# Rotary low pass of the attention scores on half the array's rows, two key chunks at a time

## The chip, the cores and the metric

One core of a Trainium2 chip runs the whole program. The metric is the device time of one execution in microseconds (us). TensorE (PE, with its weight loads PEld listed apart), VectorE (DVE), ScalarE (ACT), GpSimd (POOL) and SyncE (SP) each run their own instruction stream in order and wait for one another by semaphores.

## What is computed

The reference is a two-layer backbone over 2048 latent tokens with a prefix of 256 context tokens. Layer 0 is multi-head latent attention with 8 heads, layer 1 a Conformer convolution module. Only the scores of layer 0 matter here:

```python
NOPE_DIM, ROPE_DIM = 128, 64
q = jnp.concatenate([q_nope, q_rope], axis=-1)      # 128 + 64
k = jnp.concatenate([k_nope, k_rope], axis=-1)      # k_rope: one for all heads
s = jnp.einsum('bhqd,bhkd->bhqk', qi, k).astype(jnp.float32) * scale
p = jax.nn.softmax(s, axis=-1)
o = jnp.einsum('bhqk,bhkd->bhqd', p, v)
```

There are 2304 keys (2048 latent and 256 context) and 2048 queries for each head.

## The kernel before

The kernel works in fp32r, a reduced fp32 form, and splits each operand into a high part and a low part (what the high part leaves over); a product is then high by high, high by low and low by high. `attention` runs over 8 heads h, for each over 4 blocks j of 512 queries, and in each block over 4 query tiles i of 128. I call one (h, j) a phase. The 2304 keys are 5 chunks c: four of 512 and a last one of 256; each has its own PSUM bank `S[:, c]`.

`scores` (L831 to L848) fills one bank with five passes: three for the 128 plain dimensions (L843 to L845), and two for the rotary 64. For the latter `qr` holds the high part of the rotary query on partitions 0 to 63 and its low part on 64 to 127, and `krhi` and `krlo` hold the rotary key twice, once on each half. The pass L847, `qr` by `krhi`, thus gives high by high and low by high at once, and L848, `qr` by `krlo`, gives high by low and low by low. L848 increments `s_qk`, which says that the chunk is complete.

Phase (h, j) on TensorE makes the scores of the next phase's tile i while it transposes and multiplies the probabilities of its own. The list `slots` holds 18 key tiles and one entry `den` (the softmax denominators), and `cuts` gives 5, 5, 4 and 5 of them to the four tiles. `step` is one such entry: four transposes into one of two banks `T` (L874) and the three passes of the value product into `O` for the entry two before (L95 to L97, in the helper `split3`; the first phase's last and `den` have none). After the scores of chunk 0, 1 and 2 (only 0 and 1 in tile 2) comes one step each, and after chunk 4 two more. In tile 0 the value product of entry 0 follows chunk 3. In tile 1 a one-column product (L904) stands ahead of chunk 4.

The waits around it: `scores` of chunk c waits for `s_exp`, that is until ScalarE has taken the exponential of the previous tile's chunk c out of the same bank. `transposes` waits for `s_lo` of the entry two before, since VectorE has to have read that `T` bank.

VectorE (`phase` in its own stream) takes per tile, in this order: the maximum of chunk 0 (L1091, waits for `s_qk`), `low` of the step behind it (L1125, the low part of the transposed probabilities), the maximum of chunk 1, `low`, then the denominator of the tile before (L1110, L1112, L1117; in tile 0 the output L1134 ahead of it), the maximum of chunk 2, `low`, the maxima of chunks 3 and 4, the maximum of the five (L1098) and its negated, scaled form `nmax` (L1102); in tile 1 `q_low` follows, and then the two `low` of the tile's last two steps. ScalarE makes the high parts (`high`, L1004), waits for `nmax`, and takes the five exponentials (L988) with two `high` among them. `q_high` (L975, L976) splits the queries two phases ahead, in tile 1, and increments `s_qhi` twice.

Of the kernel before, what the change touches and what calls it, by code (L numbers as in the profile page):

```python
# [26 lines left out]
F32 = mybir.dt.float32  # L27
F32R = mybir.dt.float32r
ALU = mybir.AluOpType
ACT = mybir.ActivationFunctionType  # L30
AXX = mybir.AxisListType.X

P = 128
# [4 lines left out]
BLK = 512  # L38
NBLK = SEQ // BLK
HEADS, NOPE, ROPE, VDIM = 8, 128, 64, 128  # L40
# [11 lines left out]
NCHUNK = 5  # L52
# [6 lines left out]
def chunk(c):  # L59
    return slice(c * BLK, min((c + 1) * BLK, TOK))  # L60
# [628 lines left out]
def attention(nc, net):  # L689
# [12 lines left out]
    with nc.cleanup_on_exit(), ExitStack() as st:  # L702
        sb = lambda n, s, d=F32: st.enter_context(nc.sbuf_tensor("at_" + n, s, d))
# [5 lines left out]
        krhi, krlo = sb("krhi", [P, TOK], F32R), sb("krlo", [P, TOK], F32R)  # L709
        qst, qrst = sb("qst", [P, 2, BLK]), sb("qrst", [P, 2, BLK])  # L710
        qhi, qlo = sb("qhi", [P, 2, BLK], F32R), sb("qlo", [P, 2, BLK], F32R)
        qr = sb("qr", [P, 2, BLK], F32R)
        pthi, ptlo = sb("pthi", [P, 3, BLK], F32R), sb("ptlo", [P, 3, BLK], F32R)
        mx = sb("mx", [P, 2, 8])
        nmax = sb("nmax", [P, 2])
# [10 lines left out]
        S = st.enter_context(nc.psum_tensor("at_S", [P, NCHUNK, BLK], F32))  # L726
# [21 lines left out]
        def index(h, j):  # L748
            return h * NBH + j
# [80 lines left out]
        def _(pe):  # L830
            def scores(h, j, i, c):  # L831

                b = index(h, j)
                t = b * QT + i
                if i == 0 and c == 0:
                    pe.wait_ge(s_qlo, b + 1)
                if j == 0 and i == 0:
                    pe.wait_ge(s_klo, h * NCHUNK + (c + 1))
                if not (isinstance(t, int) and t == 0):
                    pe.wait_ge(s_exp, (t - 1) * NCHUNK + (c + 1))  # L840
                r, q, k = j % 2, slice(i * P, (i + 1) * P), chunk(c)
                out = S[:, c, 0:k.stop - k.start]
                nc.tensor.matmul(out, qhi[:, r, q], khi[:, k], start=True, stop=False)  # L843
                nc.tensor.matmul(out, qhi[:, r, q], klo[:, k], start=False, stop=False)  # L844
                nc.tensor.matmul(out, qlo[:, r, q], khi[:, k], start=False, stop=False)  # L845

                nc.tensor.matmul(out, qr[:, r, q], krhi[:, k], start=False, stop=False)  # L847
                nc.tensor.matmul(out, qr[:, r, q], krlo[:, k], start=False, stop=True).then_inc(s_qk, 1)  # L848

            def transposes(h, j, n):  # L850

# [55 lines left out]
            def phase(h, j, with_scores=True):  # L907

                nh, nj = (h, j + 1) if j + 1 < NBH else (h + 1, 0)
                for i in range(QT):  # L910
                    ns = list(range(cuts[i], cuts[i + 1]))
                    for c in range(NCHUNK):
                        if i == 1 and c == NCHUNK - 1:
                            modulation_tile(h, j)
                        if with_scores:
                            scores(nh, nj, i, c)
                        if c < len(ns) - TAIL:
                            step(h, j, ns[c])
                        if i == 0 and c == TAIL + 1:
                            values(h, j, 0)  # L920
                    for n in ns[-TAIL:]:
                        step(h, j, n)
# [13 lines left out]
            for i in range(QT):  # L936
                for c in range(NCHUNK):
                    scores(0, 0, i, c)
# [13 lines left out]
        def _(act):  # L952
# [15 lines left out]
            def q_high(h, j):  # L968
                h, j = h + j // NBH, j % NBH
                b, r = index(h, j), j % 2  # L970

                act.wait_ge(s_q[r], h * (48 * NBH // 2) + 48 * (j // 2 + 1))
                if not (isinstance(b, int) and b < 2):
                    act.wait_ge(s_qk, (b - 1) * (QT * NCHUNK))
                nc.scalar.activation(qhi[:, r], qst[:, r], ACT.Copy).then_inc(s_qhi, 1)  # L975
                nc.scalar.activation(qr[:, r], qrst[:, r], ACT.Copy).then_inc(s_qhi, 1)  # L976

            def exponential(h, j, i, c):
                b = index(h, j)
# [31 lines left out]
            def phase(h, j, last=False):  # L1011
# [3 lines left out]
                for i in range(QT):  # L1015
                    ns = list(range(cuts[i], cuts[i + 1]))
                    for c, n in enumerate(ns[:-TAIL]):
                        high(h, j, n)
                        if head_ends and i == QT - 1:
                            k_high(h + 1, c)  # L1020
                        if c == 0:
                            if j == NBH - 1 and not last and i >= 2:
                                v_high(h + 1, i - 2)
                            if j == 0 and i == 1:
                                v_high(h, VC - 1)
                    if i == 1 and (not last or j + 2 < NBH):
                        q_high(h, j + 2)
                    if i == 1 and not (isinstance(h, int) and h == 0 and j == 0):
                        store_output(*((h, j - 1) if j else (h - 1, NBH - 1)))
                    if with_scores:  # L1030
                        exponential(nh, nj, i, 0)
                    high(h, j, ns[-2])
                    if with_scores:
                        exponential(nh, nj, i, 1)
                        exponential(nh, nj, i, 2)
                    high(h, j, ns[-1])
                    if head_ends and i == QT - 1:
                        for c in range(len(ns) - TAIL, NCHUNK):
                            k_high(h + 1, c)
                    if with_scores:  # L1040
                        exponential(nh, nj, i, 3)
                        exponential(nh, nj, i, 4)

            act.wait_ge(s_krin, 16)
            nc.scalar.activation(krhi[:], prob[:, 1, 0], ACT.Copy).then_inc(s_krhi, 1)
            q_high(0, 0)
            for c in range(NCHUNK):
                k_high(0, c)
            for i in range(QT):
                for c in range(NCHUNK):  # L1050
                    exponential(0, 0, i, c)
                if i == 1:
                    q_high(0, 1)
# [14 lines left out]
        def _(dve):  # L1068
# [10 lines left out]
            def q_low(h, j):  # L1079
                h, j = h + j // NBH, j % NBH  # L1080
                b, r = index(h, j), j % 2
                dve.wait_ge(s_qhi, b * 2 + 2)
                nc.vector.tensor_tensor(qlo[:, r], qst[:, r], qhi[:, r].bitcast(F32), ALU.subtract)
                nc.vector.tensor_tensor(qr[ROPE:P, r], qrst[ROPE:P, r], qr[ROPE:P, r].bitcast(F32),
                                        ALU.subtract).then_inc(s_qlo, 1)

            def maximum(h, j, i, c):
# [48 lines left out]
            def phase(h, j, last=False):  # L1136
                nh, nj = (h, j + 1) if j + 1 < NBH else (h + 1, 0)
                with_scores = not last or j + 1 < NBH
                for i in range(QT):
# [26 lines left out]
                    if i == 1 and (not last or j + 2 < NBH):  # L1166
                        q_low(h, j + 2)
# [6 lines left out]
            dve.wait_ge(s_krhi, 1)  # L1174
            nc.vector.tensor_tensor(krlo[:], prob[:, 1, 0], krhi[:].bitcast(F32), ALU.subtract).then_inc(s_kr, 1)
            q_low(0, 0)
            for c in range(NCHUNK):
                k_low(0, c)
            for i in range(QT):
                for c in range(NCHUNK):  # L1180
                    maximum(0, 0, i, c)
                negated(0, 0, i)
                if i:
                    denominator(0, 0, i - 1)
                if i == 1:
                    q_low(0, 1)
# [794 lines left out]
def build(nc, io, out):  # L1981
    with ExitStack() as stack:
# [42 lines left out]
        latents(nc, net, "q")  # L2025
        latents(nc, net, "kv")
        attention(nc, net)
        attn_out(nc, net)
        with ExitStack() as st:
# [81 lines left out]
```

## Time and profile before

| | us |
|---|---|
| median of 3 runs | 3437.36 (3435.54 to 3441.7) |
| span of the profiled execution | 3431.4 |
| TensorE busy in the span | 3106.7 (91%) |
| VectorE busy | 1727.2 (50%) |
| ScalarE busy | 1350.7 (39%) |
| GpSimd busy | 430.7 (13%) |

The profiled execution's own time is its span and a few us around it; the median of the runs is 6.0 us above the span. The attention scores start at 774.9 us and end at 2147 us of the span. Busy time of TensorE is the sum of intervals whose ends are modelled, so the distance from one start to the next tells what a pass costs. The rows used are shown below, after the change.

### The profile page before, as it was taken

How to read it: one execution, taken by the hardware profiler on the slowest of the kernel's cores; microseconds unless marked ns; L12 is line 12 of the kernel's file. 1: busy time of each engine (PE TensorE's matmuls, PEld its weight loads, DVE VectorE, ACT ScalarE, POOL GpSimd, SP SyncE). 2: the span in 40 equal slices, each digit the busy share in tenths (PEclk: the TensorE clock that was granted, in tenths of full speed). 3: DMA queues.
4: the chain of work that ended last, by engine and by line, in shares of the span. 5: the costliest groups of instructions: out<-in, count | busy, mean ns of one | idle time of the engine just before them, and what ended most of it. 6: DMA issues, size and time to landing. Idle time of an engine off the chain costs nothing. (4 is left out here: it accounts for less than half of the span.)

```text
span 3431.4 us, 45036 instructions
## 1 busy us (share of the span) xinstructions
PE 3106.7 (91%) x15389; PEld 2574.8 (75%) x15389; DVE 1727.2 (50%) x2861; ACT 1350.7 (39%) x2896; POOL 430.7 (13%) x285
## 2 busy tenths in 40 slices
PE   7699979678999999999999999797699999996788
PEld 7588857467888787878787888686588888885666
DVE  0501134326676666676767676433533333333886
ACT  1412123345555555555555555422311111112443
POOL 1200000001111111111111111001111111112331
PEclk9799989899999999999999999998799999998899
DMA  4211133552121212121212100443222222214342
GB/s 168 82 67 71 67 120 121 184 214 72 37 65 38 66 38 66 38 66 38 66 38 66 38 32 16 160 147 123 73 70 70 66 70 68 69 51 139 106 146 99
DMA packets 216852, 285.78 MB, mean 83 GB/s; under 512 B 80561, under 2 KB 143425, under 8 KB 215489
## 3 DMA queue, kind: packets, MB, share of 16 engines
q1 hardware_dynamic: 212032, 274.76, 24.2%
q10 hardware_dynamic: 4608, 8.39, 0.7%
q8 instruction: 110, 1.80, 0.2%
q14 instruction: 102, 0.83, 0.1%
HBM read 185.04 MB, written 98.05 MB: 83 GB/s over the span
## 5 line engine op out<-in xcount | busy, mean ns | idle before, releaser
L988 ACT ACTIVATE at_prob<-at_S,at_nmax 128x512 f32<-128x512 f32 (+1 forms) x640 | 411.0, 658 | 373.3 <-DVE at_nmax L1102 354.5
L1125 DVE TENSOR_TENSOR at_ptlo<-at_T,at_pthi 128x512 fp32r<-128x512 f32 x576 | 396.4, 688 | 320.8 <-ACT at_pthi L1004 317.6
L1004 ACT ACTIVATE at_pthi<-at_T 128x512 fp32r<-128x512 f32 x576 | 348.8, 608 | 224.4 <-PE at_T L874 224.4
L1091 DVE TENSOR_REDUCE at_mx<-at_S 128x1 f32<-128x512 f32 (+1 forms) x640 | 393.2, 629 | 80.9 <-PE at_S L848 67.6
L874 PE MATMUL at_T<-ident,at_prob 128*128 128x128 f32 x2304 | 346.4, 273 | 1.6 <-DVE at_ptlo L1125 1.6
L874 PEld LDWEIGHTS at_T<-ident,at_prob 128*128 128x128 f32 x2304 | 279.0, 140 | 67.5 <-DVE at_ptlo L1125 13.1
L95 PE MATMUL ci_ps<-h1hi,ci_whi 128*128 128x512 f32 x768 | 300.2, 391 | 17.8 <-DVE ci_wlo L1553 17.8
L96 PE MATMUL ci_ps<-h1lo,ci_whi 128*128 128x512 f32 x768 | 299.8, 390 | 0.0
L97 PE MATMUL ci_ps<-h1hi,ci_wlo 128*128 128x512 f32 x768 | 299.8, 390 | 0.0
L843 PE MATMUL at_S<-at_khi,at_qhi 128*128 128x512 f32 (+1 forms) x640 | 250.2, 391 | 49.6 <-ACT at_prob L988 25.8
L95 PE MATMUL at_O<-at_pthi,at_vhi 128*128 128x512 f32 x576 | 272.8, 474 | 0.6 <-DVE at_og L1134 0.5
L847 PE MATMUL at_S<-at_krhi,at_qr 128*128 128x512 f32 (+1 forms) x640 | 239.0, 373 | 0.0
L845 PE MATMUL at_S<-at_khi,at_qlo 128*128 128x512 f32 (+1 forms) x640 | 238.1, 372 | 0.0
L848 PE MATMUL at_S<-at_krlo,at_qr 128*128 128x512 f32 (+1 forms) x640 | 238.0, 372 | 0.0
L844 PE MATMUL at_S<-at_klo,at_qhi 128*128 128x512 f32 (+1 forms) x640 | 237.4, 371 | 0.0
L97 PE MATMUL at_O<-at_pthi,at_vlo 128*128 128x512 f32 x576 | 227.6, 395 | 0.0
L96 PE MATMUL at_O<-at_ptlo,at_vhi 128*128 128x512 f32 x576 | 227.5, 395 | 0.0
L1509 ACT ACTIVATE ci_sig<-ci_ps 128x512 f32<-128x512 f32 x64 | 38.3, 598 | 429.0 <-PE ci_ps L97 429.0
L1560 DVE TENSOR_TENSOR ci_ub<-ci_ps,ci_sig 128x512 f32<-128x512 f32 x32 | 35.0, 1093 | 330.4 <-PE ci_ps L97 330.4
L95 PE MATMUL inp_ps<-h0hi,inp_whi 128*128 128x512 f32 (+1 forms) x472 | 182.1, 386 | 17.0 <-DVE inp_wlo L361 17.0
L1219 POOL TENSOR_TENSOR at_gden<-at_den,at_gst 128x512 f32<-128x512 f32 x32 | 41.3, 1291 | 1197.1 <-ACT at_den L1004 1197.1
L843 PEld LDWEIGHTS at_S<-at_khi,at_qhi 128*128 128x128 f32 x640 | 121.0, 189 | 89.2 <-ACT at_prob L988 36.7
(203 smaller groups left out, 6373.8 us busy)
## 6 DMA issues: line engine op xcount, KB each, us to landing
at_wmod<-in_w_mod SPq DMA_DIRECT2D x32, 512.0 KB, 3.6
ci_w<-in_cv_w_in SPq DMA_DIRECT2D x24, 512.0 KB, 4.2
values<-kvu_ob SPq DMA_DIRECT2D x36, 256.0 KB, 2.0
at_kst<-k_nope SPq DMA_DIRECT2D x8, 1152.0 KB, 8.0
at_vst<-values SPq DMA_DIRECT2D x8, 1152.0 KB, 7.4
mod_w<-in_w_mod SPq DMA_DIRECT2D x16, 512.0 KB, 3.5
hid_x<-in_x SPq DMA_DIRECT2D x16, 512.0 KB, 4.7
silu_gate<-inp_ob SPq DMA_DIRECT2D x32, 256.0 KB, 2.3
```

The source lines that it names most:

```text
L95: nc.tensor.matmul(out, whi, xhi, start=first, stop=False)
L96: nc.tensor.matmul(out, whi, xlo, start=False, stop=False)
L97: return nc.tensor.matmul(out, wlo, xhi, start=False, stop=last)
L843: nc.tensor.matmul(out, qhi[:, r, q], khi[:, k], start=True, stop=False)
L845: nc.tensor.matmul(out, qlo[:, r, q], khi[:, k], start=False, stop=False)
L847: nc.tensor.matmul(out, qr[:, r, q], krhi[:, k], start=False, stop=False)
L848: nc.tensor.matmul(out, qr[:, r, q], krlo[:, k], start=False, stop=True).then_inc(s_qk, 1)
L874: mm = nc.tensor.transpose(out[:, i * P:(i + 1) * P], prob[:, j % 2, i, kt * P:(kt + 1) * P], net.ident[:])
L988: nc.scalar.activation(prob[:, j % 2, i, k], S[:, c, 0:k.stop - k.start], ACT.Exp, scale=SCALE, bias=nmax[:, i % 2:i % 2 + 1], accum_out=l ...
L1004: nc.scalar.activation(dst, T[:, (n + SLOTS * j) % 2], ACT.Copy).then_inc(s_hi, 1)
L1091: nc.vector.tensor_reduce(mx[:, i % 2, c:c + 1], S[:, c, 0:k.stop - k.start], AXX, ALU.max).then_inc(s_mx, 1)
L1125: nc.vector.tensor_tensor(ptlo[:, kt % 3], T[:, (n + SLOTS * j) % 2], pthi[:, kt % 3].bitcast(F32), ALU.subtract).then_inc(s_lo, 1)
```

## The change

The rotary pass against `krlo` (L848) stays as it is for chunk 4. For chunks 0 to 3 it is left out at its place for the even chunk, and after the first four passes of the odd chunk two passes of 64 rows follow each other: the high part of the rotary query (partitions 0 to 63) by `krlo` into the even chunk's bank, and the same high part from partitions 64 to 127 by the second copy of `krlo` into the odd chunk's bank. The product low by low is no longer computed. Since `qr` holds the low part on partitions 64 to 127, a new tile `qrh` holds the high part there. ScalarE writes it with one more copy, and each of the two copies covers 64 partitions; `s_qhi` counts three to a phase.

```diff
-        qr = sb("qr", [P, 2, BLK], F32R)
+        qr, qrh = sb("qr", [P, 2, BLK], F32R), sb("qrh", [P, 2, BLK], F32R)
...
-                nc.tensor.matmul(out, qr[:, r, q], krlo[:, k], start=False, stop=True).then_inc(s_qk, 1)
+                if c == NCHUNK - 1:
+                    nc.tensor.matmul(out, qr[:, r, q], krlo[:, k], start=False, stop=True).then_inc(s_qk, 1)
+                elif c % 2:
+                    nc.tensor.matmul(S[:, c - 1], qr[0:ROPE, r, q], krlo[0:ROPE, chunk(c - 1)], start=False,
+                                     stop=True).then_inc(s_qk, 1)
+                    nc.tensor.matmul(S[:, c], qrh[ROPE:P, r, q], krlo[ROPE:P, chunk(c)], start=False,
+                                     stop=True).then_inc(s_qk, 1)
...
-                nc.scalar.activation(qr[:, r], qrst[:, r], ACT.Copy).then_inc(s_qhi, 1)
+                nc.scalar.activation(qr[0:ROPE, r], qrst[0:ROPE, r], ACT.Copy).then_inc(s_qhi, 1)
+                nc.scalar.activation(qrh[ROPE:P, r], qrst[ROPE:P, r], ACT.Copy).then_inc(s_qhi, 1)
...
-                dve.wait_ge(s_qhi, b * 2 + 2)
+                dve.wait_ge(s_qhi, b * 3 + 3)
...
-                nc.vector.tensor_tensor(qr[ROPE:P, r], qrst[ROPE:P, r], qr[ROPE:P, r].bitcast(F32),
+                nc.vector.tensor_tensor(qr[ROPE:P, r], qrst[ROPE:P, r], qrh[ROPE:P, r].bitcast(F32),
```

TensorE, in a phase, from the end of chunk 0 to the end of chunk 1, before:

```order
L847 MATMUL at_S<-at_krhi,at_qr 128x512
L848 MATMUL at_S<-at_krlo,at_qr 128x512
L874 MATMUL at_T<-ident,at_prob 128x128 x4
L95 MATMUL at_O<-at_pthi,at_vhi 128x512
L96 MATMUL at_O<-at_ptlo,at_vhi 128x512
L97 MATMUL at_O<-at_pthi,at_vlo 128x512
L843 MATMUL at_S<-at_khi,at_qhi 128x512
L844 MATMUL at_S<-at_klo,at_qhi 128x512
L845 MATMUL at_S<-at_khi,at_qlo 128x512
L847 MATMUL at_S<-at_krhi,at_qr 128x512
L848 MATMUL at_S<-at_krlo,at_qr 128x512
```

The same place in the changed kernel (its lines are one further down at first, seven from the transposes on):

```order
L848 MATMUL at_S<-at_krhi,at_qr 128x512
L881 MATMUL at_T<-ident,at_prob 128x128 x4
L95 MATMUL at_O<-at_pthi,at_vhi 128x512
L96 MATMUL at_O<-at_ptlo,at_vhi 128x512
L97 MATMUL at_O<-at_pthi,at_vlo 128x512
L844 MATMUL at_S<-at_khi,at_qhi 128x512
L845 MATMUL at_S<-at_klo,at_qhi 128x512
L846 MATMUL at_S<-at_khi,at_qlo 128x512
L848 MATMUL at_S<-at_krhi,at_qr 128x512
L852 MATMUL at_S<-at_krlo,at_qr 128x512
L854 MATMUL at_S<-at_krlo,at_qrh 128x512
```

The pass that completes chunk 0 moved from ahead of the step to behind the fourth pass of chunk 1 (L852); chunk 1 ends with L854.

VectorE keeps its order. In the changed kernel it is, from the output of tile 0 to the end of that tile, with what each row waits for:

```order
L1142 TENSOR_TENSOR at_og<-at_O,at_gden 128x512 [waits at_gden,at_mm]
L1118 TENSOR_REDUCE at_lsum<-at_lsum 128x1 [waits at_exp]
L1120 RECIPROCAL at_rl<-at_lsum 128x1 [waits at_rl]
L1125 TENSOR_SCALAR at_dg<-ident,at_rl 128x128 [waits at_recip]
L1099 TENSOR_REDUCE at_mx<-at_S 128x1 [waits at_qk]
L1133 TENSOR_TENSOR at_ptlo<-at_T,at_pthi 128x512 [waits at_hi]
L1099 TENSOR_REDUCE at_mx<-at_S 128x1 [waits at_qk] x2
L1106 TENSOR_REDUCE at_mx<-at_mx 128x1 [waits at_mx]
L1110 TENSOR_SCALAR at_nmax<-at_mx 128x1 [waits at_exp,at_mx]
```

The first L1099 here is the maximum of chunk 2. Its increment of `at_qk` came from the end of chunk 2 before and comes from L852, behind four passes of chunk 3, now; the `low` of the step (L1133) stays behind it and ahead of the maxima of chunks 3 and 4.

## Rows read from the trace of the kernel before

**Rows 1.** Busy times of one stretch; columns as named in the first line.
```profile
core 0: us, PE busy (x) PEld busy (x) DVE busy (x) ACT busy (x) POOL busy (x), PEclk, DMA share, GB/s
820.00:2100.00 1280.00, 1262.81 (x6981) 1054.46 (x6980) 892.87 (x1859) 743.44 (x1868) 173.25 (x150) 1.00 0.15 49
```

**Rows 2.** Waits from 820 to 2100 us: total us, times, longest.
```profile
ACT at_prob L988 <- DVE at_nmax L1102: 315.0, 113, 4.8
...
PEld at_S L843 <- ACT at_prob L988: 29.1, 30, 2.1
...
PEld at_T L874 <- DVE at_ptlo L1125: 9.3, 47, 0.2
```

**Rows 3.** Timeline of tile 3: start us, duration us, engine, line, operation.
```profile
1584.51 0.39 PE L848 MATMUL at_S<-at_krlo,at_qr 128*128 128x512 f32 x1
1584.51 0.19 PEld L843 LDWEIGHTS at_S<-at_khi,at_qhi 128*128 128x128 f32 x1
1584.73 0.28 PE L843 MATMUL at_S<-at_khi,at_qhi 128*128 128x256 f32 x1
...
1585.33 0.60 PE L874 MATMUL at_T<-ident,at_prob 128*128 128x128 f32 x4
...
1585.68 0.48 PE L95 MATMUL at_O<-at_pthi,at_vhi 128*128 128x512 f32 x1
...
1586.00 0.40 PE L96 MATMUL at_O<-at_ptlo,at_vhi 128*128 128x512 f32 x1
```

**Rows 4.** Timeline of VectorE over the same tile.
```profile
1581.04 0.68 DVE L1091 TENSOR_REDUCE at_mx<-at_S 128x1 f32<-128x512 f32 x1
1581.63 0.68 DVE L1125 TENSOR_TENSOR at_ptlo<-at_T,at_pthi 128x512 fp32r<-128x512 f32 x1
1582.23 0.15 DVE L1110 TENSOR_REDUCE at_lsum<-at_lsum 128x1 f32<-128x5 f32 x1
...
1582.81 0.68 DVE L1091 TENSOR_REDUCE at_mx<-at_S 128x1 f32<-128x512 f32 x1
1583.78 0.69 DVE L1125 TENSOR_TENSOR at_ptlo<-at_T,at_pthi 128x512 fp32r<-128x512 f32 x1 [0.29 <-ACT at_pthi L1004]
1584.93 1.02 DVE L1091 TENSOR_REDUCE at_mx<-at_S 128x1 f32<-128x512 f32 x2 [0.46 <-PE at_S L848]
...
1587.67 0.69 DVE L1125 TENSOR_TENSOR at_ptlo<-at_T,at_pthi 128x512 fp32r<-128x512 f32 x1 [1.33 <-ACT at_pthi L1004]
```

**Rows 5.** Timeline: the first exponential of five tiles in a row.
```profile
1543.96 0.69 ACT L988 ACTIVATE at_prob<-at_S,at_nmax 128x512 f32<-128x512 f32 x1 [2.62 <-DVE at_nmax L1102]
...
1555.11 0.69 ACT L988 ACTIVATE at_prob<-at_S,at_nmax 128x512 f32<-128x512 f32 x1 [2.95 <-DVE at_nmax L1102]
...
1565.98 0.69 ACT L988 ACTIVATE at_prob<-at_S,at_nmax 128x512 f32<-128x512 f32 x1 [1.81 <-DVE at_nmax L1102]
...
1575.69 0.69 ACT L988 ACTIVATE at_prob<-at_S,at_nmax 128x512 f32<-128x512 f32 x1 [3.30 <-DVE at_nmax L1102]
...
1586.37 0.69 ACT L988 ACTIVATE at_prob<-at_S,at_nmax 128x512 f32<-128x512 f32 x1 [2.62 <-DVE at_nmax L1102]
```

**Rows 6.** Timeline: where the next tile's first score pass started, and a step.
```profile
1576.70 0.40 PE L843 MATMUL at_S<-at_khi,at_qhi 128*128 128x512 f32 x1
...
1577.87 0.60 PE L874 MATMUL at_T<-ident,at_prob 128*128 128x128 f32 x4
...
1579.00 0.40 PE L843 MATMUL at_S<-at_khi,at_qhi 128*128 128x512 f32 x1
```

**Rows 7.** Timeline: a tile in which TensorE did wait for the exponential.
```profile
1662.75 0.69 ACT L988 ACTIVATE at_prob<-at_S,at_nmax 128x512 f32<-128x512 f32 x1 [4.71 <-DVE at_nmax L1102]
...
1663.58 0.50 PE L843 MATMUL at_S<-at_khi,at_qhi 128*128 128x512 f32 x1 [1.07 <-ACT at_prob L988]
...
1663.92 0.40 PE L844 MATMUL at_S<-at_klo,at_qhi 128*128 128x512 f32 x1
...
1664.80 0.42 PEld L874 LDWEIGHTS at_T<-ident,at_prob 128*128 128x128 f32 x4 [0.22 <-DVE at_ptlo L1125]
```

## The prediction

> **What bounds the kernel now.** I read the busy table of the attention stretch first, then the waits, then the timeline of a quiet phase tile by tile. From 820 to 2100 us TensorE is busy 1262.81 of 1280 us at a granted clock of 1.00, VectorE 892.87 and ScalarE 743.44 [rows 1]. So the stage looks like TensorE's alone, and a pass taken off its stream looks like time won. The waits say that this holds by a hair. ScalarE stands 315.0 us for the scaled maximum `nmax` before a tile's first exponential, and the weight load of the next tile's first score pass waited 30 times for that exponential, 29.1 us in all [rows 2]. The loop is: the last big chunk of scores, VectorE's maxima, `nmax`, the first exponential, and then the same PSUM bank is free for the next tile.
>
> How wide is the slack? In the tile in which TensorE did wait, the exponential started at 1662.75 and the score pass at 1663.58, with the next pass 0.34 us later instead of 0.23 [rows 7]; so a score pass can begin to stream 0.83 + 0.11 = 0.94, say 0.95 us after the start of the first exponential. In the quiet tile the exponential started at 1575.69 [rows 5] and TensorE came by itself at 1576.70 [rows 6], 1.01 us later. The slack is 0.06 us. Whatever sets the first exponential later sets TensorE later. A tile's period can then be read between first exponentials: 11.15, 10.87, 9.71 and 10.68 us for tiles 0 to 3, 42.41 us for the phase [rows 5].
>
> **What is taken from TensorE.** Five passes run from 1576.70 to 1577.87, 0.234 us each [rows 6]. Per pair of chunks two such passes (0.468) become one pair, from whose start to the next instruction's start I count p. No row shows a pass of 64 rows. p is at least one pass, 0.235, since each half still streams 512 columns; at most two in a row, 0.47. A weight load that finds no cover costs 0.09 us (the pass after the transposes takes 1585.68 to 1586.00, 0.32) [rows 3] or 0.11 [rows 7]. I take 0.34: the second half's load is not covered, its pass is. With 8 pairs in each of 32 blocks of queries, TensorE's own work shrinks by 256 x 0.13 = 33 us, at best by 60.
>
> A change of mode might cost d ahead of the pair and as much behind it. The nearest row is another change of kind, from fp32r passes to fp32 transposes, which costs nothing (1577.87 follows five even passes) [rows 6]; so d = 0. The upper end is an array that runs empty: a pass lasts 0.39 where its pitch is 0.23, and a load 0.19 [rows 3], so d = 0.16 + 0.19 = 0.35.
>
> On p, the Trainium skill ("TensorE: Matmul & The Clock Gate", Part 3, Packing small matmuls) lets tiles of different rows start some 4 ns apart; by it the pair would be 0.235 and the forecast 10 us lower. No row here shows it.
>
> **What is moved, and who stands behind it.** The even chunk is now complete only behind four passes of the odd one. VectorE serves its stream in order: maximum of chunk 2, `low`, maxima of 3 and 4. Its steps follow at 0.60 us (1581.04, 1581.63, 1582.23), the denominator takes 0.58 (to 1582.81) [rows 4]. In tile 3 the maximum of chunk 2 started at 1582.81 and `low` at 1583.78, both while TensorE still filled chunk 3; only the maxima of 3 and 4 stood behind it: 1584.93, 0.42 after the start of the last pass at 1584.51, and the exponential 1.44 after that, 1.86 in sum [rows 3 to 5]. Now the maximum of chunk 2 and the `low` behind it fall after the pair too: 0.42 + 2 x 0.60 + 1.44 = 3.06 us from the start of the pair to the exponential. That is 1.20 us more on the loop; the passes left out before it give back only part.
>
> **A second, small wait.** The step behind chunk 0 waits for the `low` of two steps before. That starts 1.30 us after the first exponential (1587.67 against 1586.37) [rows 4, 5], and the load of the transposes was released 2.05 after it (1664.80) [rows 7], so the transposes stream at 2.14. Before, five passes from 0.95 ended at 2.12. Four end at 1.88, so the pass saved in chunk 0 is lost to a wait of 0.26.
>
> **The new period**, in us from a first exponential, tile 3: scores from 0.95, transposes 2.14, a step is 1.13 (1577.87 to 1579.00) [rows 6], so chunk 1 from 3.27, pair from 4.20; chunk 2 from 4.20 + p + 1.13, chunk 3 from 7.39 + p, pair from 8.33 + p, exponential at 8.33 + p + 3.06 = 11.39 + p. VectorE is ready for it: maximum of chunk 0 at 4.63, `low` 5.23, maximum 5.83, `low` 6.43, denominator 7.03, done at 7.6, before the pair's signal at 9.1. Tile 1 is the same, 11.39 + p (its one-column product comes behind the pair). Tile 0 has no value product in the step behind chunk 2 and has it behind chunk 3, so the pair comes 0.7 earlier: 10.68 + p; the output (0.60) ends its VectorE row at 8.2, just in time. Tile 2 has one step less, and there VectorE's own row sets the end: maximum of chunk 0 at 4.70 (its start is 0.07 later, behind `q_low`), then four steps, denominator and three maxima give the exponential at 9.75, whatever p. The sum is 43.21 + 3p, with p = 0.34 it is 44.23 against 42.41: 1.82 us more per phase. With d it is 7d more, since six delays count in tiles 0, 1 and 3 and one in tile 2.
>
> 31 phases carry scores: 31 x 1.82 = 56 us. The four tiles ahead of them have no `low` between and add under 1 us. Span 3431.4 + 57 = 3488; with the 6 us by which the median stands above the span, **3494 us**. With p = 0.235 it is 3485, with 0.47 it is 3507.
>
> Costed at nothing: ScalarE's third copy in `q_high`. It stands ahead of tile 1's first exponential, where ScalarE idled 1.81 us [rows 5], and a copy is one more step of about 0.6; without that cover it would be 0.6 x 31 = 19 us. VectorE waits for it only in `q_low`, behind `nmax`. No DMA and no step of GpSimd or SyncE moves. The splits of keys and values on VectorE in the last two phases of a head are left out of the sum; [rows 7] is a tile with one, and TensorE already waited 1.07 us there. TensorE's new waits stay under 1 us each, and a wait of 1.07 us left the clock at 1.00 in that stretch [rows 1, 7], so I count no loss of clock.
>
> **Rivals.**
> *The chain has room after all* (faster). If the exponential's lateness is taken up somewhere, TensorE's saving shows: 33 us at p = 0.34, 3405; 60 at best, 3378. For it speaks the 91% of TensorE. Against it: the slack of 0.06 us, read from the very bank that is reused.
> *They cancel* (same). The chain grows by 1.20 a tile; a third or more of that would have to vanish, for instance if VectorE's queue let its work be less dense than 0.60. Then 3431 to 3444.
> *The halves run one after the other* (the change doesn't do what it says). p = 0.47, TensorE saves nothing, and the order costs what it costs: 3507.
> *A switch of mode empties the array* (slower still). With a bare load on either side, d = 0.11 and p = 0.45, the phase is 45.33, 31 x 2.92 = 91 us more: 3529. At d = 0.35 and p = 0.69 it is 47.73, 165 us more: 3602. The trace has no such switch, so nothing excludes it. The Trainium skill ("TensorEngine Tiling (Array Packing)", Key Properties) says: "Changing tiling mode (not just tile) drains the TensorE". It gives no price; it speaks for this rival, which is why I leave it a fifth.
>
> **The numbers.** The forecast (p 0.235 to 0.4, d near 0; 3480 to 3500) gets 0.40, the serial halves 0.12, the costly switch 0.22, the hidden chain 0.16, no change 0.10. A measurement of this kernel tells about 0.2% from nothing, 7 us. So slower 0.74, same 0.10, faster 0.16. The range from 3434 to 3580 leaves out the faster case and the far end of the switch.
>
> **What the profile after would show.** TensorE's pair: the start of L854 against L852 (0 to 0.11, or 0.23), and the pitch from L848 to L852 (0.23, or more with a switch). The wait of the first score pass for the exponential should appear in most tiles, some 90 of 124 or more, instead of 30. The time from L852 of chunk 3 to the first exponential should be 3.06 us. VectorE should wait about 2 us for the scores at the maxima of chunks 0 and 2 together. Short waits of the transposes for `low` should grow in number. Wrong it would be if TensorE stayed over 98% busy there with fewer passes.

## The result: 3.2% slower, and where the time went

The changed kernel takes 3545.17 us in the median (3537.72 to 3545.98), the kernel before, measured beside it, 3436.74: a ratio of 1.0316, 95% interval 1.0295 to 1.0336, 108 us. It lies inside the range, on the side that was forecast, and nearly twice as far out as the forecast of 3494 (57 us were forecast).

The page of the changed kernel, busy time and share of each engine:

```profile
span 3542.7 us, 45068 instructions
## 1 busy us (share of the span) xinstructions
PE 3194.1 (90%) x15389; PEld 2501.5 (71%) x15389; DVE 1707.8 (48%) x2861; ACT 1375.7 (39%) x2928; POOL 432.0 (12%) x285
```

The span grew by 111.3 us. The shares moved by a point or two and tell little. The attention stretch of the same length as in [rows 1], in the changed kernel, columns as there:

```profile
core 0: us, PE busy (x) PEld busy (x) DVE busy (x) ACT busy (x) POOL busy (x), PEclk, DMA share, GB/s
820.00:2100.00 1280.00, 1246.26 (x6477) 915.45 (x6476) 810.74 (x1729) 710.01 (x1756) 156.34 (x136) 0.99 0.15 47
```

The stretch now holds 6477 matmuls where it held 6981. VectorE was busy a tenth less and ScalarE a twentieth in the same 1280 us, since fewer tiles fit into them. TensorE's share went from 98.7% to 97.4%; over 98% would have spoken against the forecast. The mean granted clock is 0.99 where it was 1.00, and a paragraph below says where it fell. The waits of that stretch (total us, times, longest), to be held against [rows 2]:

```profile
ACT at_prob L996 <- DVE at_nmax L1110: 370.3, 110, 5.1
...
DVE at_mx L1099 <- PE at_S L854: 179.8, 140, 4.6
PEld at_S L852 <- issue: 79.3, 219, 0.4
PEld at_S L844 <- ACT at_prob L996: 65.1, 107, 3.1
DVE at_mx L1099 <- PE at_S L852: 58.5, 38, 2.8
PEld at_T L881 <- DVE at_ptlo L1133: 40.2, 86, 0.5
```

Four things are to be seen. TensorE's first score pass of a tile waits for the exponential 107 times instead of 30. VectorE waits for the scores 238.3 us in 110 tiles (L854 and L852), 2.2 us a tile; about 2 was forecast. Transposes wait for `low` 40.2 us instead of 9.3. And a line that was not there: the weight load of the pair's first pass, L852, stood 219 times, 79.3 us in all, 0.36 each, for nothing that another engine did.

**A tile's period.** The starts of `nmax` (L1102 before, L1110 after), one to a tile, are subtracted from each other; the table gives the mean over the third and fourth block of all eight heads, by the block and tile whose scores are made. The two middle columns are the prediction's own formula, 10.68 + p + 2d, 11.39 + p + 2d, 9.75 + d and 11.39 + p + 2d.

```
tile      before   forecast (p 0.34, d 0)   with p 0.39, d 0.20   measured
0         10.97    11.02                    11.47                 11.56
1         11.05    11.73                    12.18                 12.25
2          9.72     9.75                     9.95                  9.86
3         10.79    11.73                    12.18                 12.12
a phase   42.52    44.23                    45.78                 45.78
```

The 3.3 us a phase, 31 times, are 101 us; from the `nmax` just ahead of the first phase to the last one, 1340.7 us became 1444.4. The other 7.6 us of the 111.3 lie outside the phases, 5.0 of them in the tiles ahead of the first phase (24.6 us became 29.6 from the first `nmax` to the fourth), where the forecast had under 1. The first two blocks of a head, whose splits of keys and values the forecast left out, are not in the table: there the four tiles grew by 2.7 us (44.4 to 47.1) and by 4.3 (43.8 to 48.1).

**Where the clock fell.** In five heads TensorE stands 2.1 to 2.7 us for the exponential ahead of the first tile of the second block, where it stood 1.2 to 1.7 us before. Right behind that wait the granted clock is 0.50, the lower of its two levels (1.2 instead of 2.4 GHz). One of the five (window in us, columns as above):

```profile
1545.00:1559.10 14.10, 11.95 (x61) 8.75 (x62) 8.47 (x17) 8.59 (x22) 0.00 (x0) 1.00 0.01 2
1559.10:1562.50 3.40, 3.40 (x11) 2.71 (x11) 0.69 (x1) 2.02 (x6) 0.00 (x0) 0.50 0.04 10
```

and the rows of TensorE:

```profile
1558.84 0.59 PE L844 MATMUL at_S<-at_khi,at_qhi 128*128 128x512 f32 x1 [2.13 <-ACT at_prob L996]
1559.22 0.63 PE L845 MATMUL at_S<-at_klo,at_qhi 128*128 128x512 f32 x1
...
1562.58 0.39 PE L844 MATMUL at_S<-at_khi,at_qhi 128*128 128x512 f32 x1
```

From 1558.84 to 1562.58 it is 3.74 us; the same eight rows in the tile before, at full clock, took 2.42. The 1.3 us between them, five times, are some 7 us, an estimate. The run of the changed kernel again (e8 below) has the same tile once without the fall, behind a wait of 2.17 us: it lasted 13.02 us, and 14.53 to 15.18 in the four heads in which the clock fell. So the wait alone doesn't decide. Between 820 and 2100 us the kernel before has no such stretch.

**The pair itself.** TensorE in a tile 1 of the changed kernel, the end of chunk 1 (start us, duration, engine, line):

```profile
1574.96 0.40 PE L848 MATMUL at_S<-at_krhi,at_qr 128*128 128x512 f32 x1
1575.28 0.50 PE L852 MATMUL at_S<-at_krlo,at_qr 64*128 64x512 f32 x1
1575.29 0.50 PE L854 MATMUL at_S<-at_krlo,at_qrh 64*128 64x512 f32 x1
1575.72 0.66 PE L881 MATMUL at_T<-ident,at_prob 128*128 128x128 f32 x4
1576.13 0.48 PE L95 MATMUL at_O<-at_pthi,at_vhi 128*128 128x512 f32 x1
```

and its weight loads:

```profile
1574.73 0.19 PEld L848 LDWEIGHTS at_S<-at_krhi,at_qr 128*128 128x128 f32 x1
1575.28 0.18 PEld L852 LDWEIGHTS at_S<-at_krlo,at_qr 64*128 64x128 f32 x1 [0.36 <-issue]
1575.29 0.18 PEld L854 LDWEIGHTS at_S<-at_krlo,at_qrh 64*128 64x128 f32 x1
1575.71 0.42 PEld L881 LDWEIGHTS at_T<-ident,at_prob 128*128 128x128 f32 x4 [0.25 <-issue]
```

The two halves start 0.01 us apart: they do run side by side, loads included. But the load for L848 began together with the pass before it, and the load for L852 begins 0.32 after L848, when that pass is nearly through; so does the load of the transposes behind the pair. The first pass after a switch therefore lies 0.32 behind the last one instead of 0.23, with its load bare, 0.11 more (0.50 long instead of 0.39): d = 0.20. From there to the transposes' start is 0.44 - 0.11 = 0.33, and the transposes, whose first load is bare, take 0.41 instead of the 0.35 of [rows 3]: p = 0.39. The pair costs 0.59 where two full passes cost 0.468. The way there and back costs 0.59 - 0.235 = 0.355 us. The Trainium skill ("TensorEngine Tiling (Array Packing)", Key Properties) has the array drain at a change of mode and gives no price. The trace agrees as far as it goes: the load comes only when the pass before is nearly through (0.32 us after its start); an empty array is not in the records. The Trainium skill ("TensorE: Matmul & The Clock Gate", Part 3) also lets matmuls on different rows start about 4 ns apart. The trace agrees within the 0.01 us that its rows can tell.

### The profile page after: what moved, and what is told of

Its sections match the earlier page's. It is cut to its first block and busy times, and to the rows that moved or that the text cites. A ratio compares the mean times of both kernels' runs of the same rounds, so it can differ in the third digit from the quotient of the medians.

```text
span 3542.7 us, 45068 instructions
## 1 busy us (share of the span) xinstructions
PE 3194.1 (90%) x15389; PEld 2501.5 (71%) x15389; DVE 1707.8 (48%) x2861; ACT 1375.7 (39%) x2928; POOL 432.0 (12%) x285
## 5 line engine op out<-in xcount | busy, mean ns | idle before, releaser
L1099 DVE TENSOR_REDUCE at_mx<-at_S 128x1 f32<-128x512 f32 (+1 forms) x640 | 389.8, 631 | 284.7 <-PE at_S L854 219.1
L1133 DVE TENSOR_TENSOR at_ptlo<-at_T,at_pthi 128x512 fp32r<-128x512 f32 x576 | 394.3, 685 | 245.4 <-ACT at_pthi L1012 244.4
L881 PE MATMUL at_T<-ident,at_prob 128*128 128x128 f32 x2304 | 361.3, 279 | 9.4 <-DVE at_ptlo L1133 4.3
L881 PEld LDWEIGHTS at_T<-ident,at_prob 128*128 128x128 f32 x2304 | 264.9, 141 | 120.9 <-DVE at_ptlo L1133 52.5
L844 PE MATMUL at_S<-at_khi,at_qhi 128*128 128x512 f32 (+1 forms) x640 | 266.0, 416 | 65.4 <-ACT at_prob L996 41.9
L848 PE MATMUL at_S<-at_krhi,at_qr 128*128 128x512 f32 (+1 forms) x640 | 240.1, 375 | 0.0
L1662 POOL TENSOR_TENSOR ci_blo<-ci_tlo,ci_mask 128x640 fp32r<-128x640 f32 x64 | 109.0, 1714 | 603.9 <-DVE ci_tlo L1585 418.0
```

The costliest lines, as they stand in the source:

```text
L881: mm = nc.tensor.transpose(out[:, i * P:(i + 1) * P], prob[:, j % 2, i, kt * P:(kt + 1) * P], net.ident[:])
L1099: nc.vector.tensor_reduce(mx[:, i % 2, c:c + 1], S[:, c, 0:k.stop - k.start], AXX, ALU.max).then_inc(s_mx, 1)
L1133: nc.vector.tensor_tensor(ptlo[:, kt % 3], T[:, (n + SLOTS * j) % 2], pthi[:, kt % 3].bitcast(F32), ALU.subtract).then_inc(s_lo, 1)
```

## Experiments

Two causes are left, and the runs take them apart: the order (the even chunk is complete late, and VectorE's queue stands behind it) and the switch to 64 rows. Differences are medians against the kernel before, measured beside each group of versions (3431 to 3433 us). They are good to some 6 us (0.2%).

```
version                                        us over before   ratio, 95% interval
e1 order alone, all rows                        71               1.0204, 1.0186 to 1.0221
e2 64 rows alone, at the old place             164               1.0482, 1.0464 to 1.0500
e3 change, low ahead of the maximum             68               1.0193, 1.0175 to 1.0211
e4 one pair a tile, at the front                14               1.0040, 1.0027 to 1.0054
e5 both pairs together, one switch a tile       52               1.0154, 1.0139 to 1.0169
e6 order of chunk 0 alone, all rows             31               1.0090, 1.0072 to 1.0108
e7 order of chunk 2 alone, all rows             51               1.0143, 1.0125 to 1.0160
e8 the change again                            105               1.0309, 1.0293 to 1.0326
e9 e7 with low ahead of the maximum              6               1.0017, 1.0007 to 1.0028
e10 change, both halves on the same rows       131               1.0384, 1.0367 to 1.0402
e11 e5 with its wait between the pairs          48               1.0145, 1.0127 to 1.0162
```

### The order alone

```diff
+                if c in (0, 2):
+                    return
+                if c - 1 in (0, 2):
+                    nc.tensor.matmul(S[:, c - 1], qr[:, r, q], krlo[:, chunk(c - 1)], start=False,
+                                     stop=True).then_inc(s_qk, 1)
                 nc.tensor.matmul(out, qr[:, r, q], krlo[:, k], start=False, stop=True).then_inc(s_qk, 1)
```

> The kernel before with the order of the change alone: the rotary pass by krlo of the even chunk is put behind the four passes of the odd chunk, on all 128 rows as before, so there is no pass of 64 rows and no second mode. Theory (the late end of the even chunk lengthens the loop over VectorE and the first exponential): by the sum of the prediction with p = 0.47 and d = 0, 2.2 us a phase, some 69 us over the kernel before, 3506. Rival (only the switch to 64 rows costs): no change, 3437. Both would leave the pitch of passes at 0.23 us.

71 us measured, 69 expected. Not one pass is of another kind here, and TensorE does exactly the work it did. A tile 3 of it:

```profile
1583.01 0.39 PE L851 MATMUL at_S<-at_krlo,at_qr 128*128 128x512 f32 x1
1583.24 0.40 PE L853 MATMUL at_S<-at_krlo,at_qr 128*128 128x512 f32 x1
1583.44 0.69 DVE L1096 TENSOR_REDUCE at_mx<-at_S 128x1 f32<-128x512 f32 x1 [1.51 <-PE at_S L851]
...
1584.05 0.68 DVE L1130 TENSOR_TENSOR at_ptlo<-at_T,at_pthi 128x512 fp32r<-128x512 f32 x1
1584.64 1.01 DVE L1096 TENSOR_REDUCE at_mx<-at_S 128x1 f32<-128x512 f32 x2
1586.07 0.69 ACT L993 ACTIVATE at_prob<-at_S,at_nmax 128x512 f32<-128x512 f32 x1 [3.81 <-DVE at_nmax L1107]
```

VectorE had stood idle 1.51 us for the maximum of chunk 2; now that one and the `low` behind it come after L851, ahead of the last two maxima. From the pass to the exponential it is 1586.07 - 1583.01 = 3.06 us, the prediction's figure; before, the last big pass and the exponential lay 1.86 apart [rows 3, 5]. More than half of the loss has nothing to do with the array's rows.

### Which of the two late chunks, and what behind it

The same edit for chunk 0 alone (`c in (0,)`) and for chunk 2 alone (`c in (2,)`):

> The kernel before, all rows; only chunk 0's rotary pass by krlo is put behind the four passes of chunk 1. Theory: the late end of chunk 0 has slack on VectorE except in tile 2, but the step behind chunk 0 now comes a pass early and waits for the low of two steps before, about 0.2 us in three tiles of four: 20 to 30 us over the kernel before, 3455 to 3465. Rival (each late chunk costs the same): half of the 71 us of the version with both late, 3467.

> The kernel before, all rows; only chunk 2's rotary pass by krlo is put behind the four passes of chunk 3. Theory: the maximum of chunk 2 and the low behind it fall between the last big chunk and the exponential, 1.2 us less the pass that comes earlier: 0.97 in tile 3, 0.78 in tile 1, about 0.1 in tile 2, none in tile 0: 1.85 x 31 = 57 us over the kernel before, 3489 to 3494. Rival (each late chunk costs the same): half of the 71 us, 3467. Another rival (the order does not matter by which chunk but by the number of passes in a row on TensorE): no difference from the version with chunk 0 late.

31 and 51 us; equal halves would have been 35 each, and together they are 82, not 71. Chunk 2's is near its 57. Chunk 0's came out just above its 20 to 30, and by another way than I had it: tile 2's period went from 9.72 to 10.55 us, where the sum had 9.75. The timeline with chunk 0 late shows tile 2's start and tile 3's:

```profile
1584.36 0.69 ACT L993 ACTIVATE at_prob<-at_S,at_nmax 128x512 f32<-128x512 f32 x1 [1.80 <-DVE at_nmax L1107]
...
1586.05 0.39 PE L843 MATMUL at_S<-at_khi,at_qhi 128*128 128x512 f32 x1
...
1594.92 0.69 ACT L993 ACTIVATE at_prob<-at_S,at_nmax 128x512 f32<-128x512 f32 x1 [4.13 <-DVE at_nmax L1107]
...
1595.75 0.50 PE L843 MATMUL at_S<-at_khi,at_qhi 128*128 128x512 f32 x1 [0.49 <-ACT at_prob L993]
```

Tile 3's first pass is held by the exponential and streams 0.94 us after its start, as my sum had it for every tile. Tile 2's is not held here: it comes 1.69 us after, when TensorE is through with the steps of tile 1, and VectorE's row of tile 2 starts that much later. In the whole change tile 1's exponential is so late that the sum's 0.95 holds (1583.16 to the pass at 1584.08); tile 2 takes 9.86 us there and 9.73 with both chunks late. So tile 2's 0.8 us come only with chunk 0 late alone, and are not in the whole.

To tell the late chunk from what stands behind it, `low` goes ahead of the maximum of chunk 2:

```diff
+                        ahead = c == 2 and c < len(ns) - TAIL
+                        if ahead:
+                            low(h, j, ns[c])
                         if with_scores:
                             maximum(nh, nj, i, c)
-                        if c < len(ns) - TAIL:
+                        if c < len(ns) - TAIL and not ahead:
                             low(h, j, ns[c])
```

> The version with chunk 2 late on all rows, and on VectorE the low of the step behind chunk 2 ahead of the maximum of chunk 2. Theory: of the 50 us that the late chunk 2 cost, the part that is the low standing between the last big chunk and the exponential goes, 0.6 us in tiles 1 and 3, 37 us; what is left is the maximum of chunk 2 itself: 15 to 25 us over the kernel before, 3447 to 3456. Rival (the cost is the late chunk itself, not what stands behind it on VectorE): no change from 3482.

6 us instead of 51: the swap of two rows on VectorE takes back 45, more than the 37 us I had counted. Tiles 1 and 3 give 0.5 and 0.6 us, as counted. Tile 0 gives 0.3 more (11.02 to 10.75), and the clock, which fell to 0.50 in four heads with chunk 2 late, doesn't fall here between 820 and 2100 us. TensorE waited for the exponential 37.9 us in the stretch, against 79.2 without the swap:

```profile
PEld at_S L843 <- ACT at_prob L993: 79.2, 110, 3.0
```

with the swap:

```profile
PEld at_S L843 <- ACT at_prob L993: 37.9, 64, 1.7
```

What cost most was the in-order queue: a `low` that could have gone first stood between the late chunk's maximum and the last maxima. That the late chunk by itself costs nothing is not shown. Tile 0 is shorter than in the kernel before (10.75 against 10.97), so the swap helps there by itself, and tiles 1 and 3 are still 0.12 and 0.19 longer. The swap alone in the kernel before was not run.

The same swap in the changed kernel:

> The changed kernel with one swap on VectorE: the low of the step behind chunk 2 goes ahead of the maximum of chunk 2. Theory of the loop over VectorE: one step of 0.60 us leaves the way from the pair to the first exponential in tiles 0, 1 and 3, so up to 3 x 0.6 x 31 = 56 us less than the changed kernel, 3490, and the way from the start of the pair to the exponential falls by 0.60. Rival (TensorE's own stream with its switches is what lasts longest): no change against 3545.

68 us over before where the change, measured again, has 105: 37 us come back, not 56. Tiles 1 and 3 gave nearly the expected 0.6 each (12.25 to 11.67, 12.12 to 11.56), tile 0 gave 0.3, and tile 2 took 0.7 (9.86 to 10.54) by the shift just told: its first pass comes 1.50 us after the exponential in the mean, where it came 0.91 after. These four are 0.75 us a phase, 23 us. Much of the rest came in the second block of the heads (48.1 to 45.6 us), where the clock does not fall in this version.

### The switch alone

```diff
-                nc.tensor.matmul(out, qr[:, r, q], krlo[:, k], start=False, stop=True).then_inc(s_qk, 1)
+                if c < NCHUNK - 1:
+                    nc.tensor.matmul(out, qr[0:ROPE, r, q], krlo[0:ROPE, k], start=False, stop=True).then_inc(s_qk, 1)
+                else:
+                    nc.tensor.matmul(out, qr[:, r, q], krlo[:, k], start=False, stop=True).then_inc(s_qk, 1)
```

> The kernel before with one edit: the rotary pass by krlo of the four big chunks uses 64 rows (partitions 0 to 63), at its old place, one at a time; low by low of the rotary part is left out there. The order of completion is as before. Theory of the switch: in the changed kernel 0.76 us lay between the start of the last full pass and the start of the transposes behind the pair, 0.53 more than one pitch, and the first transposes' load was bare for another 0.06. If a lone pass of 64 rows costs the same 0.59 where a full one costs 0.234, it is 0.36 x 512 = 182 us more, 3620. Rival (a pass of 64 rows is like any other, only the order costs): 3437.

164 us, a tenth under the 182: 0.32 us for each of the 512. One chunk's end and the next one's start:

```profile
1569.84 0.39 PE L847 MATMUL at_S<-at_krhi,at_qr 128*128 128x512 f32 x1
1570.16 0.50 PE L849 MATMUL at_S<-at_krlo,at_qr 64*128 64x512 f32 x1
1570.59 0.50 PE L843 MATMUL at_S<-at_khi,at_qhi 128*128 128x512 f32 x1
1570.92 0.39 PE L844 MATMUL at_S<-at_klo,at_qhi 128*128 128x512 f32 x1
```

A lone half has the same 0.32 and 0.43 as the pair. By these rows it costs 0.38 more than a full pass (1.08 - 3 x 0.234), with an fp32r pass behind it instead of transposes. So the second half of a pair is free, and a single one costs all that the pair does.

One pair a tile, where no chunk is late by it:

```diff
+                if c == 2:
+                    if not (isinstance(t, int) and t == 0):
+                        pe.wait_ge(s_exp, (t - 1) * NCHUNK + 4)
+                    nc.tensor.matmul(S[:, 2], qr[0:ROPE, r, q], krlo[0:ROPE, chunk(2)], start=True, stop=False)
+                    nc.tensor.matmul(S[:, 3], qrh[ROPE:P, r, q], krlo[ROPE:P, chunk(3)], start=True, stop=False)
+                nc.tensor.matmul(out, qhi[:, r, q], khi[:, k], start=c not in (2, 3), stop=False)
...
```

> One pair a tile only, and at the front: the two 64-row passes of chunks 2 and 3 open their banks ahead of chunk 2, so that each chunk is complete as early as in the kernel before; chunks 0, 1 and 4 keep their full rotary pass. The loop over VectorE is untouched, so only the switch is left: a pair costs 0.59 where two passes cost 0.468. Theory of two causes: 0.12 x 128 = 15 us over the kernel before, 3452. Rival (the order is the only cost, the pair saves TensorE a pass): 0.23 x 128 = 30 us less, 3407. Rival (the 64-row passes do harm beyond their pitch): well over 3460.

14 us measured, 15 expected. With the order out of the way, a pair still loses against two full passes. The match of the totals is in part luck: tiles 0, 1 and 3 grew by 0.16, 0.17 and 0.21 us and tile 2 by 0.01, in the third and fourth blocks, not by 0.12 in each of the four. This pair has fp32r passes on both sides.

### Does the pair's length count on the path?

> The changed kernel with one edit: the second pass of each pair reads partitions 0 to 63 as the first does, so the two cannot run beside each other; the number of switches and the order are the same, and the result is the same. Theory: the pair takes one pass more, 0.23 us, and since TensorE is not what lasts longest this counts in tiles 0, 1 and 3 once each, for the pair of chunks 0 and 1: 3 x 0.23 x 31 = 21 us more than the changed kernel, 3558. Rival (TensorE's stream is what lasts longest): 256 x 0.23 = 59 us more, 3596. Rival (the halves do not really run together, their equal starts are a matter of records): no change, 3537.

131 us against 105 for the change: 25 us more, 21 expected, and not 59. The second half now starts a pass later:

```profile
1576.46 0.40 PE L848 MATMUL at_S<-at_krhi,at_qr 128*128 128x512 f32 x1
1576.78 0.50 PE L852 MATMUL at_S<-at_krlo,at_qr 64*128 64x512 f32 x1
1577.12 0.39 PE L854 MATMUL at_S<-at_krlo,at_qr 64*128 64x512 f32 x1
1577.45 0.66 PE L881 MATMUL at_T<-ident,at_prob 128*128 128x128 f32 x4
```

0.34 against 0.01, and tiles 0, 1 and 3 grew by 0.22, 0.23 and 0.25 us, although each has two pairs; tile 2 grew by 0.11, where the sum has nothing. Running side by side is worth a pass, but of the two pairs a tile only about one's length counts. By the sum it is the first one's; the second is where the path turns off to VectorE. The 25 us fit the sum's 3p a phase, and not 8p.

The changed kernel measured again:

> The changed kernel itself, on the chip of the other runs, so that the version with low ahead of the maximum and the two versions with one part of the change have a time to stand beside. Theory: 3.2% over the kernel before, as on record; the 71 us of the order alone and what the switches add (7 x 0.2 less the saving of p from 0.47 to 0.39, about 1.2 us a phase, 36 us) give 107 us over it.

105 us: the 71 of the order and 34 more with the switches, 36 expected.

### Can one switch serve two pairs?

Both pairs behind the four passes of chunk 1, the second one opening the banks of chunks 2 and 3:

```diff
+                if c == 1:
+                    if not (isinstance(t, int) and t == 0):
+                        pe.wait_ge(s_exp, (t - 1) * NCHUNK + 4)
+                    nc.tensor.matmul(S[:, 0], qr[0:ROPE, r, q], krlo[0:ROPE, chunk(0)], start=False,
+                                     stop=True).then_inc(s_qk, 1)
+                    nc.tensor.matmul(S[:, 1], qrh[ROPE:P, r, q], krlo[ROPE:P, chunk(1)], start=False,
+                                     stop=True).then_inc(s_qk, 1)
+                    nc.tensor.matmul(S[:, 2], qr[0:ROPE, r, q], krlo[0:ROPE, chunk(2)], start=True, stop=False)
+                    nc.tensor.matmul(S[:, 3], qrh[ROPE:P, r, q], krlo[ROPE:P, chunk(3)], start=True, stop=False)
...
```

> Both pairs of a tile stand together behind the four passes of chunk 1: the pair of chunks 0 and 1 ends them, the pair of chunks 2 and 3 opens those. One switch to 64 rows a tile instead of two, and only chunk 0 is complete late. Theory of two causes: the switch costs 0.355 whatever follows, a pair 0.235, so the two pairs take 0.83 where four full passes took 0.94: 0.11 x 128 = 14 us less on TensorE; against it the late chunk 0 makes the transposes wait 0.2 and VectorE's row in tile 2 end some 0.2 later. In all 3425 to 3450 against 3432 to 3437 before, and less than the version with one pair in front. Rival (each pair of passes costs by itself, not the switch): 2 x 0.12 x 128 = 31 us over the kernel before, 3463 or more.

A miss: 52 us over the kernel before, where I had a draw. The pairs behave as priced:

```profile
1567.12 0.40 PE L851 MATMUL at_S<-at_krhi,at_qr 128*128 128x512 f32 x1
1567.45 0.50 PE L855 MATMUL at_S<-at_krlo,at_qr 64*128 64x512 f32 x1
1567.45 0.50 PE L857 MATMUL at_S<-at_krlo,at_qrh 64*128 64x512 f32 x1
1567.79 0.39 PE L859 MATMUL at_S<-at_krlo,at_qr 64*128 64x512 f32 x1
1567.80 0.39 PE L860 MATMUL at_S<-at_krlo,at_qrh 64*128 64x512 f32 x1
1568.12 0.66 PE L888 MATMUL at_T<-ident,at_prob 128*128 128x128 f32 x4
```

From L851 to L888 it is 1.00, less the pitch of L851 and with the 0.06 of the transposes 0.83, against 0.94 for four full passes. So TensorE does save 0.11 us a tile, and the kernel is slower all the same. My first explanation was the wait for the bank of chunk 3, which I had put ahead of both pairs; its row in the waits is

```profile
PEld at_S L855 <- ACT at_prob L1003: 32.2, 83, 0.7
```

The wait was moved between the pairs:

> The version with one switch a tile, with the wait for the banks of chunks 2 and 3 put between the two pairs instead of ahead of both, so that the pair of chunks 0 and 1 does not stand behind it. Theory: that version lost 31 us by the late chunk 0, as measured alone, and about 32 us by this wait (83 waits in the trace), against 14 us less on TensorE; with the wait behind the first pair some 25 us come back: 3450 to 3462. Rival (two pairs in a row cost more than their pitch shows): no change from 3484.

48 us over before instead of 52, a difference within the noise, although that wait is gone from the trace: the explanation falls. The periods say where it is: tile 2 takes 10.55 us (9.72 before), the same as with chunk 0 late on all rows, and the first four tiles of a head, with splits of values on VectorE, take 47.3 us together (44.4 before, 45.1 with chunk 0 late). The late chunk 0 explains the first. The other is 2.2 us, 15 us in seven heads, and the traces show three parts of it. In tile 2 a split of values takes VectorE 2.02 us beside work of GpSimd, where it takes 0.95 in the version with only chunk 0 late; with both pairs together:

```profile
1511.36 2.02 DVE L1092 TENSOR_TENSOR at_vlo<-at_vst,at_vhi 128x768 fp32r<-128x768 f32 x1
```

with chunk 0 late alone:

```profile
1501.19 0.95 DVE L1082 TENSOR_TENSOR at_vlo<-at_vst,at_vhi 128x768 fp32r<-128x768 f32 x1
```

That tile grows from 11.2 to 12.2 us, about 7 us in seven heads. In tile 3 TensorE then waits 2.31 us for the exponential instead of 1.61, and in five heads the clock falls to 0.50 behind that wait. The tile takes 11.27 us in a head without the fall (11.04 with chunk 0 late) and 12.5 to 12.6 with it: 0.2 us by the wait, some 2 us in all, and 1.3 by the clock, five times, some 6. Why the split is so long beside GpSimd's work is not shown.

No version was faster than the kernel before.

## Why the forecast was right in its way and short in size

- **What bounds the kernel.** Right: with the order changed and nothing else, 71 us were lost while TensorE's work stayed the same. But the slack of 0.06 us was read from one tile and holds for tile 3. Over the third and fourth blocks the first score pass of tiles 0 to 3 came 1.23, 1.04, 1.68 and 1.01 us after the exponential before it, so the slack is 0.28, 0.09, 0.73 and 0.06 us against 0.95. In the change it comes 0.83 to 0.91 after and has its load bare, so the slack is used up in all four, and the sum's start at 0.95 holds for each. With chunk 0 alone late it did not, which is where the 31 us came from by another way than expected.
- **What is moved.** Right, and to the size: 3.06 us from the pass to the exponential in tiles 1 and 3 of the version with the order alone. In the change it is 3.17 (L852 at 1553.14, exponential at 1556.31), the 0.11 of the bare load more:

```profile
1553.14 0.50 PE L852 MATMUL at_S<-at_krlo,at_qr 64*128 64x512 f32 x1
...
1556.31 0.69 ACT L996 ACTIVATE at_prob<-at_S,at_nmax 128x512 f32<-128x512 f32 x1 [4.01 <-DVE at_nmax L1110]
```

- **The second, small wait.** Right: transposes waited for `low` 86 times, 40.2 us, before 47 times and 9.3 us.
- **The switch, d.** This is the term that was mis-sized, and the main one: d was taken as 0 from the change between fp32r passes and fp32 transposes [rows 6], which costs nothing, and measured 0.20. That row was near in place and not in kind, since both of its sides use all 128 rows. With 7d a phase it is 7 x 0.20 x 31 = 43 us. p was 0.39 instead of 0.34, by the bare load behind the pair, 3 x 0.05 x 31 = 5 us. 3494 + 48 = 3542 is the measured time within 3 us. That it is so near is in part luck: the sum has neither the 5.0 us ahead of the phases nor the falls of the clock, and the growth of the first two blocks (2.7 and 4.3 us) only happens to have a mean near that of the quiet ones (3.3). The upper bound of 0.35 holds; it took 0.16 + 0.19 us for an array that runs empty and a bare load, where the rows show 0.09 and 0.11.
- **p.** The reason given was wrong where its value was near: I left the second half's load uncovered; it is covered, and what is bare is the load of the first half and that of the instruction behind the pair.
- **The clock.** Counted at nothing, on the ground that new waits stay under 1 us. They reach 2.1 to 2.7 us in the first tile of the second block, and the clock fell behind five of them, some 7 us by the estimate above.
- **The rivals.** *The chain has room after all* and *they cancel* are out: the order alone costs 71 us. *The halves run one after the other* is out: 0.01 us apart, and forced apart they cost 25 us more. *A switch of mode empties the array* is what happened on top of the forecast's own mechanism, between the two prices that I gave it (3529 at d = 0.11, 3602 at 0.35).
- **ScalarE's third copy** cost nothing that shows: ahead of tile 1's exponential it still idles 2.33 us in the changed kernel. No run takes the copy out.

## What to carry to other kernels

Before an edit moves the end of one product behind the next, read what the consumer's queue holds behind it: an engine that serves in order turns one late signal into all the steps up to the one that matters. Here a swap of two of them was worth 45 us where one chunk was late. A busy share of 98.7% on one engine doesn't say that its time is what counts, if another engine's chain closes the same loop with 0.06 to 0.7 us to spare; read that slack in every kind of tile, not in one. A longer wait can cost twice when the clock falls behind it. Packing products of 64 rows onto both halves of the array saves TensorE time here only from the second pair per switch on (0.83 against 0.94 us), and no version turned that into a faster kernel.

## What the runs showed of the hardware

Products on the two halves of the array's rows start 0.01 us apart, weight loads included, and the second is free; a lone one costs as much as the pair (0.32 and 0.43 us to and from its start in both). Going from 128 rows to 64 and back costs 0.355 us in all: the weight loads did not begin under the pass before (0.36 and 0.25 us of idle ahead of them). With an fp32r pass behind instead of transposes it is 0.38 by the rows, and 0.32 by the time of the run with 512 lone passes. A second pair in the same mode adds 0.24 us, about a full pass. From fp32r passes to fp32 transposes, both on all rows, there is no such price, and on the way back 0.09 us for the bare load [rows 3, 6].

Behind waits of TensorE of 2.1 to 2.7 us the granted clock went from 1.00 to 0.50 in five heads of the changed kernel; behind one of 2.17 us in its second run it did not, and behind those of up to 1.7 us in the same tile of the kernel before it did not. A subtraction of 128x768 on VectorE took 0.95 us, and 2.02 beside work of GpSimd.
